# Fifteen half-size groups instead of twelve, the plain down products behind them, and the table sums as accumulating transfers

## The chip, the core and the metric

One core of a Trainium2 chip runs the whole program: TensorE (PE) multiplies, VectorE (DVE), ScalarE (ACT) and GpSimd (POOL) prepare and take away, SyncE (SP) and ACT issue transfers. The metric is the device time of one execution in microseconds. The kernel before takes 3717.69 us (median of 3 runs, 3717.36 to 3717.88).

## The reference, cut to what matters

Two encoder layers over 512 tokens of width 1024. Each has a token mixer (Fourier branch, attention, gates), which the change leaves alone, and a retrieval layer of 16,384 single-neuron experts, which it touches:

```python
def peer_ffn(x, w_query, sub_keys, u_tab, v_tab):
    ...
        q = (xc @ w_query).reshape(-1, PEER_HEADS, 2, PEER_HALF)
        ...
        gate = jax.nn.softmax(sv, axis=-1)
        u = u_tab[eidx]
        act = jax.nn.gelu(jnp.einsum('thkd,td->thk', u, xc), approximate=False)
        w = gate.astype(act.dtype) * act
        vv = v_tab[eidx]
        return jnp.einsum('thk,thkd->td', w, vv)
...
x = layer_norm(DEEPNORM_ALPHA * x + y_p, ln2_g[l], ln2_b[l])
```

## The kernel before, in words

The experts are computed densely. The gates of all heads are summed into a dense array (token by expert), which goes to DRAM. Then, for 32 groups of 512 experts, the kernel forms u·x ("up"), applies gelu, multiplies by the gates ("weights" of the group) and multiplies by the rows of v ("down"), which are added into X. Every 32-bit operand is split into a high and a low part, and a product is three matmuls: high by high, high by low, low by high (`product`, L1561 to L1563). POOL makes the low parts of the tables (L506), the high parts too where nobody else does (L518); in the stages around the gates ACT makes the high parts. A table "piece" is 1 MB; two landing tiles and two pairs `part_h`, `part_l` are used in turn, each in two halves.

Order of one layer's expert work on PE:

1. Early up products (`early_product`): their gelu goes to DRAM (`early_acts`). There are EG = 18 groups of them, 36 pieces: 16 before the dense gates, 16 woven into them (`dense_gates`, 8 blocks), and 4 after them (E_AFTER).
2. Plain down products of 17 of those 18 groups: DVE multiplies `acts_in` by `gate` (`weigh`, L1337), ACT rounds (L846), DVE takes the low part (L1341), PE does 2 halves of 48 matmuls, and DVE adds each pair of banks into X (`add_up`, L1358). The first such group multiplies X by alpha in the same instruction (L1355).
3. One group with up and down products, then SG = 12 "seven" groups (`seven_group`): the up product of the next group, and a down product by Winograd's variant of Strassen's scheme: the 512 x 512 by 512 x 1024 product is cut in blocks of half size, and seven products (P1, P2, P3, P5, P4, P7, P6) of 12 matmuls each take the place of eight. The four sums of table blocks are made by POOL (`table_sum`, L559) in `vraw`, in place; the sums of the weights by DVE. Results go to X or to four accumulators `acc` (`add_seven`, L1443).
4. `gather_seven` adds the accumulators into X in eight steps (L1491, L1494), beside the up product of one more group; the last down product and the layer norm follow.

Everything is in program order on each engine and tied by counting semaphores (`Tally`); `used` counts pieces that PE is through with, `y_added` the bank pairs that DVE has added, `t_added` the table sums, `s_bank` the weight banks that are free again.

Of the kernel before, what the change touches and what calls it, by code (L numbers as in the profile page):

```python
# [5 lines left out]
F32 = mybir.dt.float32  # L6
# [7 lines left out]
P = 128  # L14
# [18 lines left out]
CG = 4  # L33
# [7 lines left out]
EG = 18  # L41
E_BEFORE, E_AFTER = 16, 4
E_WITHIN = 2 * EG - E_BEFORE - E_AFTER
# [19 lines left out]

SG = NG - EG - 2
S_FIRST = P_UV + 4
S_UV = S_FIRST + 2 * SG
S_LAST = S_UV + 4
NS = S_LAST + 2
assert SG % 2 == 0 and NS == NP - 2 * SG
# [49 lines left out]
def build(nc, x, stream, keys, ln0, ln1, ln2, qk_gain, gate_bias, consts, out):  # L119
    ctx = ExitStack()  # L120
    with ctx:
# [97 lines left out]
        raw_h = overlay("raw_h", 56, [P, 2, 3, 2, HALF], F32R)  # L219
        raw_l = overlay("raw_l", 68, [P, 2, 3, 2, HALF], F32R)  # L220
# [3 lines left out]
        end_h = [overlay(f"end_h{i}", kib, [P, CG, S], F32R) for i, kib in enumerate((0, 80))]  # L224
        end_l = [overlay(f"end_l{i}", kib, [P, CG, S], F32R) for i, kib in enumerate((8, 88))]
# [21 lines left out]
        Wh = overlay("Wh", 16, [P, 2, CG, S], F32R)  # L247
        Wl = overlay("Wl", 32, [P, 2, CG, S], F32R)
        gate = [overlay(f"gate{i}", 48 + 8 * i, [P, S, CG]) for i in range(2)]
        acts_in = [overlay(f"acts_in{i}", 72 + 8 * i, [P, CG, S]) for i in range(2)]  # L250
# [75 lines left out]
        spilled = [tally(f"spilled{i}", 0, 16 * S // 64) for i in range(2)]  # L326
        gate_in = [tally(f"gate_in{i}", 0, 16 * n) for i, n in enumerate((EG // 2 + NG - EG, EG // 2))]
# [17 lines left out]
        t_added = tally("t_added", 0, 4 * SG)  # L345
# [5 lines left out]
        seven_added = tally("seven_added", 7, 7 * SG)  # L351
        acc_zero = tally("acc_zero", 0, 1)
# [77 lines left out]
        def _(sp):  # L430
# [11 lines left out]
            def rounds(first, end, sevens):  # L442
                with sp.Fori(first, end) as r:
                    for s in range(LANDINGS):

                        sp.wait_ge(split.sem, r * (2 * LANDINGS) + 2 * (s - LANDINGS + 1 - 2 * SG * sevens))
                        sp.dma_start(landing[s][:], flat[r * LANDINGS + s]).then_inc(landed[s], 16)
# [10 lines left out]
            def seven_pieces(l):  # L458
# [10 lines left out]
                sp.wait_ge(used.sem, used.at(l, P_UV))  # L469
                down_piece(0, 0)  # L470
                up_piece(0, 0)
                down_piece(0, 1)
                up_piece(0, 1)
                with sp.Fori(0, SG - 1) as k:
# [5 lines left out]
                    down_piece(k + 1, 1)  # L480

            begin = 1
            for l in range(DEPTH):
                rounds(begin, (l * NP + P_OUT) // LANDINGS, l)
                for n in range(2):
                    wide_rows(l, n)
                rounds((l * NP + P_OUT + 4) // LANDINGS, (l * NP + P_UV + 4) // LANDINGS, l)
                seven_pieces(l)
                begin = (l * NP + V_LAST - 4) // LANDINGS
# [1617 lines left out]
```

## Time and profile before

| | us |
|---|---|
| median of the runs | 3717.69 |
| the profiled execution: its own time | 3718.94 |
| its span, first to last instruction | 3716.7 |
| PE busy | 3671.4 (99%) |
| POOL busy | 2498.0 (67%) |
| DVE busy | 2526.1 (68%) |
| ACT busy | 1150.8 (31%) |

Layer 0's expert work runs as follows: dense gates until 844, plain down products to about 1263, seven groups to 1790, the rest to 1850; layer 1 repeats it 1846 us later. Busy shares say who works; who is waited for has to be read from the waits and from the timeline of single instructions. The records of matmuls overlap, so a matmul's cost is read from the distance of two starts, not from its length.

### The profile page before, as it was taken

To read this page: it belongs to the slowest core of one execution; us is meant where nothing else is said; L and a number is where in the kernel's file an instruction comes from. 1 tells how busy PE (TensorE), PEld (TensorE's weight loads), DVE (VectorE), ACT (ScalarE), POOL (GpSimd) and SP (SyncE) were. 2 spreads that over 40 slices of the span, in tenths; PEclk is the share of its full clock that TensorE was granted. 3 is DMA by queue.
4 is the path that set the end of the run, shared out by engine and by line. 5 is a ranking of instruction groups with operands and counts; after the bars stand their busy time and mean duration, and the time that the engine had idled before them with its cause. 6 is when DMAs were issued, how large, how long until landed. Compare 5 with 4: busy or idle time off the path is not lost.

```text
span 3716.7 us, 53645 instructions
## 1 busy us (share of the span) xinstructions
PE 3671.4 (99%) x18336; PEld 3032.3 (82%) x18336; DVE 2526.1 (68%) x4281; ACT 1150.8 (31%) x1725; POOL 2498.0 (67%) x1124
## 2 busy tenths in 40 slices
PE   8999999999999999999999999999999999999998
PEld 7778888888888888888887788888888888888886
DVE  7545999994777555555675469999857775555546
ACT  1651134541111134444125412344511111444431
POOL 6445554336777699999764455543377776999995
PEclk9999999999999999999999999999999999999999
DMA  4122245886545433333221223368865553334332
GB/s 154 69 69 103 103 144 176 244 247 247 206 183 192 158 125 113 130 148 117 91 104 69 80 92 113 139 192 243 245 244 191 195 200 136 114 133 148 113 124 79
DMA packets 230084, 555.03 MB, mean 149 GB/s; under 512 B 10048, under 2 KB 141376, under 8 KB 181440
## 3 DMA queue, kind: packets, MB, share of 16 engines
q1 hardware_dynamic: 47968, 337.14, 25.6%
q10 hardware_dynamic: 181984, 216.17, 17.3%
q8 instruction: 78, 1.28, 0.1%
q14 instruction: 54, 0.44, 0.0%
HBM read 446.32 MB, written 106.95 MB: 149 GB/s over the span
## 4 chain that ended last, share of the span: by engine, by line
PE 94%; DVE 3%; POOL 2%; issue 1%; ACT 0%; DMA 0%; POOLq 0%; DVEq 0%; ACTq 0%
PE bank L1561 29%; PE bank L1562 29%; PE bank L1563 29%; PE bank L1890 2%; PE bank L1891 2%; POOL part_l L506 1%; PE bank L1687 1%; PE bank L1850 1%; PE bank L1675 1%; POOL part_h L518 1%; DVE X L1013 1%; DVE X L1015 1%; PE bank L1666 0%; PE bank L1667 0%; DVE stats L999 0%
## 5 line engine op out<-in xcount | busy, mean ns | idle before, releaser
L506 POOL TENSOR_TENSOR part_l<-landing,part_h 128x1024 fp32r<-128x1024 f32 x536 | 1414.6, 2646 | 531.4 <-ACT part_h L766 454.7
L1561 PE MATMUL bank<-XTh,part_h 128*128 128x512 f32 (+1 forms) x2688 | 1047.4, 390 | 5.3 <-ACT Gf L661 2.9
L1563 PE MATMUL bank<-XTh,part_l 128*128 128x512 f32 (+1 forms) x2688 | 1034.1, 385 | 0.0
L1562 PE MATMUL bank<-XTl,part_h 128*128 128x512 f32 (+1 forms) x2688 | 1034.0, 385 | 0.0
L518 POOL TENSOR_SCALAR part_h<-landing 128x1024 fp32r<-128x1024 f32 x316 | 418.1, 1323 | 598.1 <-PE bank L1563 456.5
L1561 PEld LDWEIGHTS bank<-XTh,part_h 128*128 128x128 f32 x2688 | 505.2, 188 | 104.1 <-ACT Gf L661 3.8
L1563 PEld LDWEIGHTS bank<-XTh,part_l 128*128 128x128 f32 x2688 | 505.1, 188 | 101.6
L1562 PEld LDWEIGHTS bank<-XTl,part_h 128*128 128x128 f32 x2688 | 505.6, 188 | 95.5
L552 POOL TENSOR_TENSOR part_l<-vraw,part_h 128x1024 fp32r<-128x1024 f32 x168 | 420.4, 2529 | 42.7 <-ACT part_h L897 42.7
L1561 PE MATMUL bank<-part_h,Wh 128*128 128x512 f32 x1152 | 448.1, 389 | 0.0
L1562 PE MATMUL bank<-part_l,Wh 128*128 128x512 f32 x1152 | 448.1, 389 | 0.0
L1563 PE MATMUL bank<-part_h,Wl 128*128 128x512 f32 x1152 | 448.1, 389 | 0.0
L1337 DVE TENSOR_TENSOR bank<-acts_in,gate 128x512 f32<-128x512 f32 x144 | 302.2, 2144 | 66.0 <-DMA acts_in<-early_acts 58.6
L1358 DVE TENSOR_TENSOR X<-X,bank 128x512 f32<-128x512 f32 x288 | 184.1, 681 | 209.9 <-PE bank L1563 209.9
L846 ACT CAST Wh<-bank 128x512 fp32r<-128x512 f32 x144 | 84.4, 588 | 657.6 <-DVE bank L1337 649.1
L1562 PEld LDWEIGHTS bank<-part_l,Wh 128*128 128x128 f32 x1152 | 216.2, 188 | 45.2
L1563 PEld LDWEIGHTS bank<-part_h,Wl 128*128 128x128 f32 x1152 | 216.2, 188 | 44.8
L1561 PEld LDWEIGHTS bank<-part_h,Wh 128*128 128x128 f32 x1152 | 216.2, 188 | 44.7
L897 ACT CAST part_h<-vraw 128x1024 fp32r<-128x1024 f32 x168 | 170.9, 1044 | 248.4 <-POOL vraw L559 198.5
L755 ACT ACTIVATE early<-bank 128x512 f32<-128x512 f32 x144 | 86.3, 599 | 367.8 <-PE bank L1563 327.1
L1380 DVE TENSOR_TENSOR bank<-bank,gate 128x512 f32<-128x512 f32 x64 | 69.2, 1084 | 188.0 <-ACT bank L870 188.0
L559 POOL TENSOR_TENSOR vraw<-vraw,vraw 128x1024 f32<-128x1024 f32 x72 | 192.0, 2666 | 3.4
(214 smaller groups left out, 5904.0 us busy)
## 6 DMA issues: line engine op xcount, KB each, us to landing
landing<-stream SPq DMA_DIRECT2D x268, 1024.0 KB, 4.8
dense_gates<-spill ACTq DMA_DIRECT2D x32, 2048.0 KB, 9.3
gate<-dense_gates ACTq DMA_DIRECT2D x64, 1024.0 KB, 5.1
vraw<-stream SPq DMA_DIRECT2D x48, 1024.0 KB, 5.1
early_acts<-early ACTq DMA_DIRECT2D x144, 256.0 KB, 2.5
acts_in<-early_acts ACTq DMA_DIRECT2D x36, 1024.0 KB, 7.5
LNP<-ln ACTq DMA_DIRECT2D x4, 1024.0 KB, 5.9
X<-x SPq DMA_DIRECT2D x4, 512.0 KB, 7.3
```

The source lines that it names most:

```text
L506: nc.gpsimd.tensor_tensor(halves(part_l[s], h), halves(landing[s], h), halves(part_h[s], h).bitcast(F32), ALU.subtract).then_inc(split.sem, 1)
L518: nc.gpsimd.tensor_scalar(halves(part_h[s], h), halves(landing[s], h), 1.0, 0.0, ALU.mult, ALU.add).then_inc(high_part.sem, 1)
L552: nc.gpsimd.tensor_tensor(unit(part_l, i), block_of(*UNIT_BLOCK[i]), unit(part_h, i).bitcast(F32), ALU.subtract).then_inc(v_low.sem, 1)
L559: nc.gpsimd.tensor_tensor(block_of(*out), block_of(*left), block_of(*right), ALU.subtract).then_inc(t_added.sem, 1)
L755: nc.scalar.activation(early[:, slot, :], bank[slot][:], ACT.Gelu).then_inc(early_out.sem, 1)
L846: nc.scalar.copy(Wh[:, par, c, :], bank[first_bank + c][:]).then_inc(w_high.sem, 1)
L897: nc.scalar.copy(unit(part_h, i), block_of(*UNIT_BLOCK[i])).then_inc(v_high.sem, 1)
L1337: nc.vector.tensor_tensor(w, acts_in[par][:, c, :], gate[par][:, :, c], ALU.mult).then_inc(w_full.sem, 1)
L1358: ins = nc.vector.tensor_tensor(xs, xs, new, ALU.add)
L1561: nc.tensor.matmul(dst, sth, mvh, start=first, stop=False)
L1562: nc.tensor.matmul(dst, sth, mvl, start=False, stop=False)
L1563: return nc.tensor.matmul(dst, stl, mvh, start=False, stop=last)
```

## The change

EG becomes 16, E_AFTER goes, SG becomes 15. After the dense gates PE does the up product of the first seven group, then the fifteen seven groups, then all 17 plain down products (the group whose up product came last, the 16 early ones). The gates' first load, the alpha scaling of X (now four ACT instructions) and the seven groups' first tables come right behind the dense gates. The four table sums become DMAs from POOL with `accum_op=ALU.add`; so that all are additions, ACT turns the sign of two table blocks (`turn_over`), and P2 and P5 are subtracted instead of added. `gather_seven` is split in four parts of two steps, one behind each of the first four plain groups; `add_up` and `down` take the banks in the order 6, 7, 4, 5.

```diff
-EG = 18
-E_BEFORE, E_AFTER = 16, 4
+EG = 16
+E_BEFORE = 16
...
-SG = NG - EG - 2
+SG = NG - EG - 1
...
-                def table_sum(n, lows, out, left, right):
+                def table_sum(n, lows, out, new):
                     pool.wait_ge(v_low.sem, v_low.at(l, 7 * k + lows))
-                    if n > 1:
-                        pool.wait_ge(t_added.sem, t_added.at(l, 4 * k + n - 1))
-                    nc.gpsimd.tensor_tensor(block_of(*out), block_of(*left), block_of(*right),
-                                            ALU.subtract).then_inc(t_added.sem, 1)
+                    if n == 1:
+                        pool.wait_ge(turned.sem, turned.at(l, 2 * k + 2))
+                    else:
+                        pool.wait_ge(t_added.sem, t_added.at(l, 64 * k + 16 * (n - 1)))
+                    pool.sem_inc(went_on, 1)
+                    pool.dma_start(block_of(*out), block_of(*new), accum_op=ALU.add).then_inc(t_added.sem, 16)
...
                 down_low(P1)
                 down_low(P2)
-                pool.wait_ge(v_landed[1].sem, v_landed[1].at(l, 16 * k + 16))
-                table_sum(1, P1 + 1, b11, b12, b11)
-                table_sum(2, P1 + 1, b12, b22, b12)
+                table_sum(1, P1 + 1, b11, b12)
                 down_low(P3)
+                table_sum(2, P3 + 1, b12, b22)
                 down_low(P5)
+                table_sum(3, P3 + 1, b22, b11)
                 up_lows(1)
-                table_sum(3, P3 + 1, b22, b22, b11)
-                table_sum(4, P3 + 1, b21, b22, b21)
+                table_sum(4, P3 + 1, b21, b22)
...
-                for k in range(2):
-                    act.dma_start(gate[k][:], dense[k]).then_inc(gate_in[k].sem, 16)
-                    act.dma_start(acts_in[k][:], ...).then_inc(acts_back[k].sem, 16)
-                for i in range(E_AFTER - 1):
-                    early_piece(E_BEFORE + E_WITHIN + i, 0, True)
+                act.dma_start(gate[0][:], dense[EG]).then_inc(gate_in[0].sem, 16)
+                for slot in range(4):
+                    act.wait_ge(early_saved[slot].sem, early_saved[slot].at(l, 16 * EG))
+                for tb in range(TB):
+                    ins = nc.scalar.activation(X[:, tb, :], X[:, tb, :], ACT.Copy, scale=ALPHA)
+                ins.then_inc(scaled.sem, 1)
...
+                    def turn_over(chunk, half):
+                        block = block_of(chunk, half)
+                        nc.scalar.activation(block, block, ACT.Copy, scale=-1.0).then_inc(turned.sem, 1)
...
                     act.wait_ge(v_landed[0].sem, v_landed[0].at(l, 16 * k + 16))
+                    turn_over(1, 0)
                     down_high(P1)
+                    act.wait_ge(turned.sem, turned.at(l, 2 * k + 1))
                     down_high(P2)
                     activate(k + 1, 0, None)
                     act.wait_ge(v_landed[1].sem, v_landed[1].at(l, 16 * k + 16))
+                    turn_over(0, 1)
                     down_high(P3)
...
-                gather_seven()
...
+                seven_group(SG - 1, 0, True)
+                dve_group(0, 0, (v_low.sem, v_low.at(l, 7 * SG)))
+                gather_seven(0, (0, 1))
+                dve_group(1, 1, (used.sem, used.at(l, S_DOWN + 2)))
+                gather_seven(1, (2, 3))
+                for q in (2, 3):
+                    dve_group(q, q - 2, (used.sem, used.at(l, S_DOWN + 2 * q)))
+                    gather_seven(q, (2 * q, 2 * q + 1))
...
-                down_group(0, 0, P_VA, [])
-                with pe.Fori(0, EG // 2 - 1) as m:
-                    down_group(2 * m + 1, 1, 4 * m + (P_VA + 2))
-                    down_group(2 * m + 2, 0, 4 * m + (P_VA + 4))
-                pe.wait_ge(early_out.sem, early_out.at(l, CG * EG))
-                both_group(EG - 1, Wh[:, 1], Wl[:, 1], P_UV, ...)
+                for half in range(2):
+                    up(half, S_UP + half, half, lambda c: (early_out.sem, early_out.at(l, CG * EG)))
                 with pe.Fori(0, SG // 2) as m:
                     for par in range(2):
                         seven_group(2 * m + par, par)
-                both_group(EG, end_h[0], end_l[0], S_UV, ...)
+                seven_group(SG - 1, 0)
+                down_group(0, end_h, end_l, [(seven_added.sem, seven_added.at(l, 7 * SG - 1 + n)) for n in range(2)])
+                down_group(1, Wh[0], Wl[0])
+                with pe.Fori(1, EG // 2) as m:
+                    for par in (1, 0):
+                        down_group(2 * m + (1 - par), Wh[par], Wl[par])
```

POOL in a seven group before (vraw0 holds blocks b11 and b21, vraw1 holds b12 and b22; a row with `part_l` is a low part, one with `vraw` on the left a table sum):

```order
L552 TENSOR_TENSOR part_l1<-vraw0_98,part_h1 128x1024 [waits v_high]
L567 ISA
L559 TENSOR_TENSOR vraw0_98<-vraw1_99,vraw0_98 128x2x512 [waits v_low,v_landed1]
L559 TENSOR_TENSOR vraw1_99<-vraw1_99 128x2x512 [waits t_added,v_low]
...
L552 TENSOR_TENSOR part_l0<-vraw0_98,part_h0 128x1024 [waits v_high]
...
L506 TENSOR_TENSOR part_l1<-landing1,part_h1 128x1024 [waits u_high]
L559 TENSOR_TENSOR vraw1_99<-vraw1_99,vraw0_98 128x2x512 [waits t_added,v_low]
L559 TENSOR_TENSOR vraw0_98<-vraw1_99,vraw0_98 128x2x512 [waits t_added,v_low]
```

The same place now:

```order
L571 TENSOR_TENSOR part_l1<-vraw0_98,part_h1 128x1024 [waits v_high]
L577 ISA [waits v_low]
L581 DMA vraw0_98<-vraw1_99 128x2x512 [waits turned]
...
L571 TENSOR_TENSOR part_l0<-vraw1_99,part_h0 128x1024 [waits v_high]
L579 ISA [waits v_low]
L581 DMA vraw1_99<-vraw1_99 128x2x512 [waits t_added]
...
L571 TENSOR_TENSOR part_l0<-vraw0_98,part_h0 128x1024 [waits v_high]
L579 REGISTER_ALU [waits v_low]
L581 DMA vraw1_99<-vraw0_98 128x2x512 [waits t_added]
...
L581 DMA vraw0_98<-vraw1_99 128x2x512 [waits t_added]
```

Each sum now stands behind a wait for the transfer before it, with POOL's own low parts between them.

DVE at the second of the plain groups behind the seven groups, now (rows `X<-X,bank` are `add_up`, `bank<-acts_in,gate` are `weigh`, rows with `acc` on the right the gathering); it starts with the last pair of banks of the group before:

```order
L1367 TENSOR_TENSOR X<-X,bank4 128x512 [waits used]
L1367 TENSOR_TENSOR X<-X,bank5 128x512
...
L1505 TENSOR_TENSOR acc3_103<-acc3_103,acc0_100 128x1024 [waits y_added,seven_added]
L1505 TENSOR_TENSOR acc2_102<-acc2_102,acc3_103 128x1024 [waits acc_step]
L1350 TENSOR_TENSOR bank0<-acts_in1_128,gate1_126 128x512 [waits acc_step,used,acts_back1,gate_in1]
L1350 TENSOR_TENSOR bank1<-acts_in1_128,gate1_126 128x512
...
L1354 TENSOR_TENSOR Wl1_124<-bank0,Wh1_122 128x512 [waits w_high]
...
L1367 TENSOR_TENSOR X<-X,bank6 128x512 [waits v_first,y_added]
```

In a plain group before nothing stood between the two kinds of rows:

```order
L1358 TENSOR_TENSOR X<-X,bank 128x512 x2
L1337 TENSOR_TENSOR bank<-acts_in_126,gate_124 128x512 x2
L1340 ISA
L1341 TENSOR_TENSOR Wl<-bank,Wh 128x512
L1340 ISA
L1341 TENSOR_TENSOR Wl<-bank,Wh 128x512
```

Two gathering rows now stand ahead of the first `weigh` of each of four groups, and the add of banks 6 and 7 stands behind that `weigh`.

## Rows read from the trace of the kernel before

**Rows 1.** The page: busy time, share and instructions of each engine.

```profile
PE 3671.4 (99%) x18336; PEld 3032.3 (82%) x18336; DVE 2526.1 (68%) x4281; ACT 1150.8 (31%) x1725; POOL 2498.0 (67%) x1124
```

**Rows 2.** Waits of PE: line, waited for: us in total, times, longest.

```profile
PE bank L1574 <- DMA C<-consts: 12.2, 1, 12.2
...
PE bank L1561 <- POOL part_l L506: 2.9, 6, 0.9
```

**Rows 3.** Stretches: PE, PEld, DVE, ACT, POOL busy, clock, DMA share, GB/s.

```profile
900.00:1270.00 370.00, 370.00 (x1634) 306.39 (x1633) 264.32 (x268) 39.95 (x68) 288.99 (x137) 1.00 0.51 186
1300.00:1785.00 485.00, 485.00 (x2141) 401.62 (x2140) 254.16 (x395) 197.02 (x248) 444.26 (x179) 1.00 0.33 123
```

**Rows 4.** Timeline, PE, a seven group's start: start, us, what.

```profile
1504.90 0.39 PE L1561 MATMUL bank<-XTh,part_h 128*128 128x512 f32 x1
...
1515.78 0.39 PE L1561 MATMUL bank<-part_h,raw_h 128*128 128x512 f32 x1
```

**Rows 5.** Timeline, POOL, the same group.

```profile
1506.44 5.69 POOL L552 TENSOR_TENSOR part_l<-vraw,part_h 128x1024 fp32r<-128x1024 f32 x2 [0.54 <-ACT part_h L897]
...
1526.46 5.73 POOL L559 TENSOR_TENSOR vraw<-vraw,vraw 128x1024 f32<-128x1024 f32 x2
1533.36 7.13 POOL L552 TENSOR_TENSOR part_l<-vraw,part_h 128x1024 fp32r<-128x1024 f32 x3 [1.16 <-ACT part_h L897]
```

**Rows 6.** Timeline, ACT, the same group.

```profile
1505.32 2.00 ACT L897 CAST part_h<-vraw 128x1024 fp32r<-128x1024 f32 x2 [1.88 <-PE bank L1563]
1510.54 0.58 ACT L870 ACTIVATE bank<-bank 128x512 f32<-128x512 f32 x1 [3.22 <-PE bank L1563]
```

**Rows 7.** DMA issues: count, KB each, median us to landing.

```profile
landing<-stream SPq DMA_DIRECT2D x268, 1024.0 KB, 4.8
...
vraw<-stream SPq DMA_DIRECT2D x48, 1024.0 KB, 5.1
...
out<-X SPq DMA_DIRECT2D x4, 512.0 KB, 2.7
```

**Rows 8.** Timeline, ACT, end of the dense gates of layer 0.

```profile
844.14 0.60 ACT L755 ACTIVATE early<-bank 128x512 f32<-128x512 f32 x1 [2.17 <-PE bank L1563]
...
845.53 0.39 ACTq L818 DMA_DIRECT2D dense_gates<-spill  x1
...
855.22 0.36 ACTq L836 DMA_DIRECT2D gate<-dense_gates  x1
855.61 0.46 ACTq L837 DMA_DIRECT2D acts_in<-early_acts  x1
```

**Rows 9.** Timeline, DVE, the same place.

```profile
863.67 2.05 DVE L1337 TENSOR_TENSOR bank<-acts_in,gate 128x512 f32<-128x512 f32 x2 [29.00 <-DMA acts_in<-early_acts]
```

**Rows 10.** Timeline, DVE, one half of a plain down group.

```profile
1061.74 1.28 DVE L1358 TENSOR_TENSOR X<-X,bank 128x512 f32<-128x512 f32 x2 [2.88 <-PE bank L1563]
1062.94 4.27 DVE L1337 TENSOR_TENSOR bank<-acts_in,gate 128x512 f32<-128x512 f32 x2
1067.12 1.44 DVE L1341 TENSOR_TENSOR Wl<-bank,Wh 128x512 fp32r<-128x512 f32 x2
1068.48 1.28 DVE L1358 TENSOR_TENSOR X<-X,bank 128x512 f32<-128x512 f32 x2
```

**Rows 11.** Timeline, DVE, the gathering behind the seven groups.

```profile
1792.02 1.42 DVE L1494 TENSOR_TENSOR acc<-acc,acc 128x1024 f32<-128x1024 f32 x1
1793.47 1.96 DVE L1491 TENSOR_TENSOR X<-X,acc 128x1024 f32<-128x1024 f32 x1
1795.35 3.41 DVE L1491 TENSOR_TENSOR acc<-acc,acc 128x1024 f32<-128x1024 f32 x1
1798.68 12.70 DVE L1491 TENSOR_TENSOR X<-X,acc 128x1024 f32<-128x1024 f32 x5
```

**Rows 12.** Timeline, DVE, a seven group's weights times gates.

```profile
1511.15 0.62 DVE L1389 TENSOR_TENSOR sum_of<-bank,gate 128x256 f32<-128x256 f32 x1 [3.63 <-ACT bank L870]
...
1516.59 1.10 DVE L1380 TENSOR_TENSOR bank<-bank,gate 128x512 f32<-128x512 f32 x1 [3.83 <-ACT bank L870]
...
1520.35 0.42 DVE L1403 TENSOR_TENSOR sum_of<-sum_of,bank 128x256 f32<-128x256 f32 x1
```

More of the change, by code:

```diff
@@ L467, in down_piece, with plain_piece @@
                                  flat[4 * k + (l * NP + P_UV + 5 + 2 * s)]).then_inc(v_landed[s].sem, 16)
[L469 to L473, printed above, removed]
+                def plain_piece(n, s, piece):
+                    sp.wait_ge(split.sem, split.at(l, 2 * (n + s - LANDINGS + 1)))
+                    sp.dma_start(landing[s][:], flat[l * NP + piece]).then_inc(landed[s], 16)
+                for s in range(2):
+                    plain_piece(S_UP, s, P_UV + 2 * s)
+                for s in range(2):
+                    up_piece(0, s)
+                for s in range(2):
+                    sp.wait_ge(spilled[s].sem, spilled[s].at(l, 16 * (S // 64)))
+                for s in range(2):
+                    down_piece(0, s)
                 with sp.Fori(0, SG - 1) as k:
@@ L614, in xt_parts @@
                                    bank[banks[i]][:].rearrange("p (k t) -> p k t", k=4)).then_inc(xt_high.sem, 1)
+            for k in range(2):
+                act.sem_inc(spilled[k].sem, 16)
             root(1, slice(0, 2))
@@ L1461, in seven_group @@
                     if last:
[L1462 removed]
+                        end_lows(0)
                     else:
@@ L1514, in _ @@
-                dve.wait_ge(used.sem, used.at(l, P_UV))
+                    dve.wait_ge(seven_added.sem, seven_added.at(l, 7 * SG))
+                    dve.wait_ge(y_added.sem, y_added.at(l, 4 * group + 4))
+                    for n in steps:
+                        dst, new = [(p6, p1), (p7, p6), (x11, p1), (x12, p6), (x21, p7), (x22, p7), (x12, p5),
+                                    (x22, p5)][n]
+                        if n > 0:
+                            dve.wait_ge(acc_step.sem, acc_step.at(l, n))
+                        nc.vector.tensor_tensor(dst, dst, new, ALU.add).then_inc(acc_step.sem, 1)
@@ L1515, in _ @@
+                    dve.wait_ge(acc_step.sem, acc_step.at(l, steps[-1] + 1))
+                    dve.sem_inc(went_on, 1)
+                for k in range(2):
+                    dve.wait_ge(spilled[k].sem, spilled[k].at(l, 16 * (S // 64)))
+                for i in range(4):
+                    ins = nc.vector.memset(acc[i][:], 0.0)
+                ins.then_inc(acc_zero.sem, 1)
                 for p in range(2):
```

298 lines of the change are left out of this document (120 added, 178 removed).

## The prediction, made before the run

> **What bounds the kernel now.** I read the page's busy times first: PE is busy 99% of the span, no other engine over 68% [rows 1]. Then PE's waits: the longest is the start's wait for the constants, and for POOL's low parts it waits 2.9 us in all [rows 2]. Then the stretches: in the plain down products and in the seven groups alike PE is busy all the time at the full granted clock, while POOL works 92% of the seven groups' stretch (444 of 485 us) and 78% of the plain one's (289 of 370), and DVE 52% and 71% [rows 3]. So the end is set by PE's row of matmuls, and a change pays by the matmuls that it takes away, as long as every operand keeps arriving in time. The timelines of single instructions are for that second half: how early each operand is there.
>
> **What it removes.** From one seven group's first up matmul (1504.90) to its first P1 matmul (1515.78) are 48 matmuls: 10.88 / 48 = 0.2267 us each [rows 4]. A plain down product has 96 of them, a seven group's has 7 x 12 = 84. Three more groups in each of two layers take away 3 x 2 x 12 = 72 matmuls: 16.3 us. Up products and everything else on PE keep their number.
>
> **The four sums as transfers, in a group that runs steadily.** Times from here count from the group's first up matmul. PE does up (48 matmuls) to 10.9, P1, P2, P3 and P5 (2.72 each) to 21.8, up again to 32.65, then P4, P7 and P6 to 40.8. P4 needs the fourth sum. Before, POOL had the sums done at 27.3 (1526.46 + 5.73) and the low part of P4 at about 30.9 [rows 5], 1.8 us ahead of need. Now ACT first turns a block, 1.0 us like its cast of the same size, so P1's cast ends at 0.42 + 2.0 = 2.4 [rows 6]. Two low parts of 2.4 follow on POOL (7.13 for three in a row [rows 5]), and the second turn, behind the gelu that starts at 5.6, ends at 7.2 [rows 6]: the first sum is issued at 7.4. Each later one is issued when the one before has landed. From the fourth landing to P4's low part it is a cast and a low part, 3.5 with the hand-overs. With L for a transfer from issue to landing, 0.4 for the hand-overs, and 1.5 more for the fourth, which meets the landing of the next 1 MB piece, the condition is 7.4 + 4L + 1.9 + 3.5 <= 32.65, so L <= 4.96 us. Every us above costs 4 us in each of 30 groups, 120 us. Nothing like this transfer is in the trace of before. The nearest rows are 512 KB written out in 2.7 us and 1 MB loaded in 4.8 and 5.1 [rows 7]. An accumulating transfer must read the new block and the old one, 1 MB, and write 512 KB. The bounds are 2.7 (it costs nothing) and something above 5.1 by POOL's own issue: I put 6 as the upper end, one of the 1 MB rows and some 0.9 for an issue that no row shows. I take 4.8, the row nearest to it in bytes read. Then P4 is ready at 32.0, 0.65 us ahead: nothing in the steady group. Lower ends below zero are excluded, since PE does not wait there now. The up product's second piece is next: POOL comes to its low part after the third issue, 7.4 + 2 x 4.9 + 1 = 18.2, and has it at 20.6, needed at 21.8. The freed time of POOL (4 x 2.4 us in each group) buys nothing, since nobody waited for POOL. ACT's two turns are 2 us of 40.8 on an engine that was busy 41% [rows 3] and are hidden but for the place counted above. P5's low part ends at 7.4 + 4.8 + 3.5 = 15.8, needed at 19.05.
>
> The Trainium skill ("DMA: Bandwidth & Descriptors", Anatomy of one DMA) gives for a POOL-issued DMA 2.0 us plus bytes over 436 GB/s; with 1 MB read that is an estimate of 4.4 us, inside the budget, and the forecast stays. The same page's table (Bandwidth, measured) has 6.15 us of transfer time alone for 1 MB on that path, which no run here shows yet; by it the steady group would be 4.8 us late and the kernel some 143 us slower than my sum, the first rival below.
>
> **Behind the dense gates.** Before, four early pieces (43.5 us of PE) covered the way of the gates to DRAM and back. Now PE has 96 matmuls, 21.8 us. Layer 0, absolute times:
> - The up product waits for all early gelus. The last starts at 844.14 and takes 0.60 [rows 8]: PE stands from about 843.95 to 844.9, 0.95 us, and is through with both up pieces at 866.7.
> - The spill is issued at 845.53 and its landing lets the gate load go at 855.22 [rows 8], the same now. With it SP now issues two `vraw` loads of 1 MB, which need the same landing. Before, the second of the four loads issued there took from 855.61 to 863.6 (DVE's wait ends at 863.67 [rows 9]), so I let the gate land at 863.4; alone it would be at 860.3. The alpha scalings of X, 4 x 1.0 on ACT, end at 859.7 and lie beside that, and so do the memsets.
> - DVE then needs 2 x 0.62 for the first chunk, 1.10 for the second and four sums of 0.42 [rows 12], 4.0; high and low parts of the bank on ACT and DVE take it to 869.4 (2.0, from casts and low parts of 0.4 to 0.7 for such sizes, half of the 1.44 for two in [rows 10]). PE stands 2.7 us.
> - The first seven group lacks its lead: the second pair of chunks takes ACT and DVE until 877, only then come turn, cast and low part of P1, ready at 881.8 where PE wants it at 880.3 (1.5 us). The first sum is issued at 884.3, that is 14.9 after the group's start instead of 7.4. P3 costs 0.5 more, P5 (landing 889.1, ready 892.6) 2.2, the second up piece (behind the third issue) 2.1, P4 1.4: 7.7 us. In the next group the lag is gone.
> That is 11.4 us a layer. The lower end is 1.5 (gate at 860.3, L of 2.7), the upper 18 (L of 6).
>
> **The gathering inside the plain groups.** In a plain half DVE starts with the last pair of banks at 1061.74, weighs (4.27), takes low parts, and has added the next pair at 1068.48 + 1.28 = 1069.8, when PE wants it at 1061.6 + 10.88 = 1072.5 [rows 10]: 2.7 us of slack. Two gathering steps now stand ahead of that. They took 1.42 and 3.41 for the accumulators, 1.96 and 12.70 / 5 = 2.54 for X [rows 11]: 4.8, 4.5, 5.1 and 5.1 for the four pairs. PE then waits 2.1, 1.8, 2.4 and 2.4 us for banks 6 and 7 in the middle of four groups: 8.7 us a layer. If the steps run at the 1.42 of the quickest, it is 0.1 each; if all at 3.41, 16. Before, they lay beside an up product that needed none of these banks. PE's first plain group has 1.4 us to the second half of its first table piece, like the up product before; I count no difference.
>
> **The sum.** Own time of the profiled execution 3718.94 (span 3716.7 and 2.2 around it), -16.3, +2 x 11.4, +2 x 8.7: 3742.8. That execution is 1.25 above the median, so 3742. This measurement can tell a change from none at about 0.2%, 7.4 us.
>
> **Rivals.**
> 1. *The transfers are too slow.* L of 5.8 (1 MB load and an issue): P4 is late by 4 x 0.84 = 3.4 us in 30 groups, 101 us: 3843. For it: four in a row that each wait for the one before, in a group that had 1.8 us to spare. Against it: three of the four lie where no load is in flight. It decides from 4.96 us. The 6.15 of the page named above would give 3885.
> 2. *The covers hold, and it is faster.* DVE and POOL slow each other now (a low part takes 2.4 alone, 3.3 beside DVE [rows 5]); if POOL, freed of the sums and standing between pieces, leaves the gathering at 1.42 a step, and L is near the 2.7 of the 512 KB row, then what is left is 0.95 + 0.5 behind the gates and 0.4 of gathering in each layer: 3718.9 - 16.3 + 3.7 - 1.25 = 3705. It decides where waits come to under 8.9 us in all (16.3 - 7.4).
> 3. *Half of it.* The steps are as quick as in 2 but the first seven group starts late as I count it, or the reverse: 16 us of waits, 3718.
>
> **How the numbers follow.** Forecast 0.37, own range 3728 to 3758; rival 1 0.32; rival 2 0.20; rival 3 0.11. Faster by over 0.2%: 0.20; within: 0.11; slower: 0.69. The range leaves out the last us of rival 2 and the part of rival 1 above L of 5.8: 3706 to 3840.
>
> **What would show it.** Right: PE's waits name ACT's early gelu (0.9 a layer), DVE's `raw_l` (2 to 3) and POOL's `part_l` from `vraw` (some 8 a layer, all in the first group); in the middle of four plain groups PE waits about 2 us for DVE's add of banks 6 and 7; seven groups still follow each other every 40.8 us; the POOL transfers land in 4.4 to 5.0 us. Wrong: a period above 40.9 (rival 1, and the landing time gives it), no wait in the gathering groups, or a gate that lands within 5 us of its issue.

## The result and the profile after

The changed kernel takes 3957.72 us (median of 4 runs, 3957.36 to 3964.36), the kernel before 3717.53 beside it (3716.99 to 3717.88): a ratio of 1.065, 95% interval 1.063 to 1.067. It is 240 us slower. I had forecast 3742 and a range up to 3840, so the time lies outside. The profile is that of the slowest of the four executions (3964.36).

The page's first part of the changed kernel (busy us, share, instructions), which answers to [rows 1]:

```profile
PE 3745.0 (95%) x18264; PEld 3061.4 (77%) x18264; DVE 2609.1 (66%) x4389; ACT 1284.4 (32%) x1871; POOL 2332.3 (59%) x1118
```

PE has the 72 matmuls less that I counted (18336 to 18264), and yet its busy time rises by 74 us: some matmuls take longer. Its share falls from 99% to 95%. The waits of PE (total us, times, longest), which answer to [rows 2]:

```profile
PE bank L1555 <- POOL part_l L571: 118.9, 32, 4.0
PE bank L1555 <- POOL part_l L525: 30.1, 38, 4.6
PE bank L1555 <- DVE X L1367: 22.6, 8, 2.9
...
PE bank L1555 <- DVE raw_l L1421: 5.5, 2, 2.9
...
PE bank L1555 <- ACT early L775: 1.4, 2, 0.7
```

L571 is the low part of a block of v (plain or summed), L525 that of an up piece, L1367 the adding of banks to X. The first row has 32 waits for 30 groups: one for P4 in every seven group, which I had forecast free of waits in the steady group, and two for P5 in the first group of each layer. A stretch of the seven groups of layer 0 (PE, PEld, DVE, ACT, POOL, clock, DMA share, GB/s), which answers to the second of [rows 3]:

```profile
1100.00:1200.00 100.00, 87.17 (x362) 70.39 (x362) 46.58 (x71) 40.97 (x51) 64.78 (x32) 0.95 0.55 147
```

PE stands 13 of 100 us, with POOL down from 92% to 65%, and the clock below 1.00 for the first time. One group of those, on POOL (start, us, what, idle time before), which answers to [rows 5]; PE begins this group at 1113.80:

```profile
1116.29 4.77 POOL L571 TENSOR_TENSOR part_l<-vraw,part_h 128x1024 fp32r<-128x1024 f32 x2 [1.49 <-ACT part_h L909]
1121.56 1.20 POOL L581 DMA_DIRECT2D vraw<-vraw  x1 [0.50 <-POOL part_l L571]
1122.33 2.84 POOL L571 TENSOR_TENSOR part_l<-vraw,part_h 128x1024 fp32r<-128x1024 f32 x1
1127.17 1.20 POOL L581 DMA_DIRECT2D vraw<-vraw  x1 [2.00 <-DMA vraw<-vraw]
1127.95 2.87 POOL L571 TENSOR_TENSOR part_l<-vraw,part_h 128x1024 fp32r<-128x1024 f32 x1
1132.76 1.20 POOL L581 DMA_DIRECT2D vraw<-vraw  x1 [1.95 <-DMA vraw<-vraw]
1133.54 5.19 POOL L525 TENSOR_TENSOR part_l<-landing,part_h 128x1024 fp32r<-128x1024 f32 x2
1138.32 1.57 POOL L581 DMA_DIRECT2D vraw<-vraw  x1
1148.97 7.03 POOL L571 TENSOR_TENSOR part_l<-vraw,part_h 128x1024 fp32r<-128x1024 f32 x3 [9.07 <-ACT part_h L909]
```

The four rows of L581 are the transfers. They are issued 5.61, 5.59 and 5.56 us apart, each when the one before has landed. The fourth is issued at 1138.32, and what it lets go on ACT starts only 9.5 us later. SP's queue and ACT's timeline of the same group:

```profile
1138.90 0.33 SPq L470 DMA_DIRECT2D landing<-stream  x1
```

```profile
1147.83 1.99 ACT L909 CAST part_h<-vraw 128x1024 fp32r<-128x1024 f32 x2 [14.92 <-DMA vraw<-vraw]
```

SP issued the next 1 MB piece 0.58 us behind the fourth transfer. On PE, same group:

```profile
1147.23 0.39 PE L1557 MATMUL bank<-XTh,part_l 128*128 128x512 f32 x1
1151.46 0.79 PE L1555 MATMUL bank<-part_h,raw_h 128*128 128x512 f32 x1 [3.83 <-POOL part_l L571]
1152.05 0.63 PE L1556 MATMUL bank<-part_l,raw_h 128*128 128x512 f32 x1
1152.47 0.63 PE L1557 MATMUL bank<-part_h,raw_l 128*128 128x512 f32 x1
...
1156.59 0.39 PE L1555 MATMUL bank<-part_h,sum_h 128*128 128x512 f32 x1
```

P4 starts at 1151.46, where PE wanted it at 1147.46, and then its twelve matmuls start 0.43 us apart instead of 0.23. The same stretch by windows (columns as above):

```profile
1147.60:1151.40 3.80, 0.02 (x1) 0.00 (x0) 1.06 (x2) 3.57 (x5) 2.43 (x2) 0.76 0.00 0
1151.50:1156.20 4.70, 4.70 (x11) 3.74 (x12) 2.71 (x5) 0.25 (x1) 4.49 (x2) 0.50 0.58 223
1156.50:1162.00 5.50, 5.50 (x26) 4.54 (x25) 3.69 (x6) 3.80 (x5) 3.75 (x2) 1.00 0.85 328
```

After PE stood for 3.8 us the granted clock is 0.50, that is 1.2 GHz, for 4.7 us, and then 1.00 again. A late operand costs twice: the wait of 4.0, and the slow matmuls (1151.46 to 1156.59 is 5.13 for twelve starts instead of 12 x 0.2267 = 2.72), 2.4. In 8 of the 30 groups all twelve matmuls are slow like this; in the other 22 it is seven or eight of them, some starting only after a few at full rate, 1.6 us. Over the 30 groups that is 54 us. With 0.9 for the up product's second piece this group is some 7 us too long: groups of layer 0 begin at 923.17 and, six later, at 1209.62, so one takes 47.7, against the 40.8 of before.

The DMA rows of the changed kernel, which answer to [rows 7] (count, KB each, median us to landing):

```profile
landing<-stream SPq DMA_DIRECT2D x256, 1024.0 KB, 5.0
...
gate<-dense_gates ACTq DMA_DIRECT2D x64, 1024.0 KB, 6.3
vraw<-stream SPq DMA_DIRECT2D x60, 1024.0 KB, 4.9
vraw<-vraw POOLq DMA_DIRECT2D x120, 512.0 KB, 5.0
```

The median of 5.0 is that of three in four. The fourth is told by the timeline alone.

### The profile page after: what moved, and what is told of

Same layout as the page of the kernel before. It is cut to its first block and busy times, and to the rows that moved or that the text cites. A ratio compares the mean times of both kernels' runs of the same rounds, so it can differ in the third digit from the quotient of the medians.

```text
span 3962.4 us, 53991 instructions
## 1 busy us (share of the span) xinstructions
PE 3745.0 (95%) x18264; PEld 3061.4 (77%) x18264; DVE 2609.1 (66%) x4389; ACT 1284.4 (32%) x1871; POOL 2332.3 (59%) x1118
## 5 line engine op out<-in xcount | busy, mean ns | idle before, releaser
L525 POOL TENSOR_TENSOR part_l<-landing,part_h 128x1024 fp32r<-128x1024 f32 x512 | 1354.2, 2678 | 550.6 <-ACT part_h L786 456.6
L571 POOL TENSOR_TENSOR part_l<-vraw,part_h 128x1024 fp32r<-128x1024 f32 x210 | 525.0, 2514 | 337.4 <-ACT part_h L909 337.4
L537 POOL TENSOR_SCALAR part_h<-landing 128x1024 fp32r<-128x1024 f32 x268 | 347.9, 1298 | 570.4 <-PE bank L1557 423.5
L1555 PE MATMUL bank<-part_h,Wh 128*128 128x512 f32 x1024 | 402.9, 394 | 23.5 <-DVE X L1367 22.6
L1557 PE MATMUL bank<-part_h,Wl 128*128 128x512 f32 x1024 | 401.5, 392 | 0.0
L1556 PE MATMUL bank<-part_l,Wh 128*128 128x512 f32 x1024 | 401.4, 392 | 0.0
L909 ACT CAST part_h<-vraw 128x1024 fp32r<-128x1024 f32 x210 | 212.5, 1039 | 497.3 <-DMA vraw<-vraw 497.3
L1367 DVE TENSOR_TENSOR X<-X,bank 128x512 f32<-128x512 f32 x256 | 163.1, 681 | 170.1 <-PE bank L1557 170.0
L1555 PE MATMUL bank<-part_h,raw_h 128*128 128x512 f32 x360 | 163.2, 453 | 114.1 <-POOL part_l L571 114.1
L1555 PEld LDWEIGHTS bank<-part_h,Wh 128*128 128x128 f32 x1024 | 194.0, 189 | 68.3 <-issue 25.9
L1451 DVE TENSOR_TENSOR acc<-acc,bank 128x512 f32<-128x512 f32 x240 | 154.1, 683 | 132.4 <-PE bank L1557 132.4
L581 POOL DMA_DIRECT2D vraw<-vraw x120 | 154.3, 1286 | 132.3 <-DMA vraw<-vraw 118.9
L1557 PEld LDWEIGHTS bank<-part_h,Wl 128*128 128x128 f32 x1024 | 194.0, 189 | 40.8
```

What stands on the lines that cost most here:

```text
L525: nc.gpsimd.tensor_tensor(halves(part_l[s], h), halves(landing[s], h), halves(part_h[s], h).bitcast(F32), ALU.subtract).then_inc(split.sem, 1)
L537: nc.gpsimd.tensor_scalar(halves(part_h[s], h), halves(landing[s], h), 1.0, 0.0, ALU.mult, ALU.add).then_inc(high_part.sem, 1)
L571: nc.gpsimd.tensor_tensor(unit(part_l, i), block_of(*UNIT_BLOCK[i]), unit(part_h, i).bitcast(F32), ALU.subtract).then_inc(v_low.sem, 1)
L581: pool.dma_start(block_of(*out), block_of(*new), accum_op=ALU.add).then_inc(t_added.sem, 16)
L909: nc.scalar.copy(unit(part_h, i), block_of(*UNIT_BLOCK[i])).then_inc(v_high.sem, 1)
L1367: ins = nc.vector.tensor_tensor(xs, xs, new, ALU.add)
```

## The experiments

Theory A: the transfers make nearly all of the loss, as a chain, and within it the fourth, which shares the DMA engines with SP's load. Theory B (the main rival): it is the order around them, the fifteenth group and what stands behind the gates. Each run computes the whole reference. Times are medians; a ratio is against the kernel before, run beside it (medians of 3717.4 to 3718.3).

**The load behind the fourth transfer.** SP waits for the fourth sum before it loads the up piece's second half.

```diff
                     up_piece(k + 1, 0)
+                    sp.wait_ge(t_added.sem, t_added.at(l, 64 * k + 64))
                     up_piece(k + 1, 1)
```

> The changed kernel, with SP's load of the next group's second up piece held back until the fourth table sum has landed. Theory A (the fourth transfer takes 9.5 us instead of 5.0 because that 1 MB load is issued in the same microsecond and shares the DMA engines): the fourth lands in 5 to 6 us, P4's low part is there 3.8 us earlier, PE's wait for it falls to 0.5 us or less, the slow matmuls behind it go too, and a seven group takes 41 to 41.5 us instead of 47.6: 3957.7 less some 30 x 6.2 = 3770 to 3790 us. Theory B (the fourth is slow by itself, for its blocks or its place behind POOL's low parts): it still lands after 9.5 us, a group stays at 47.6 us and the time within 10 us of 3957.7.

3799.96 us, ratio 1.022 (1.020 to 1.024): 157.8 us less, 10 us short of what theory A gave. Timelines of POOL, ACT and SP of that run:

```profile
1025.90 1.52 POOL L582 DMA_DIRECT2D vraw<-vraw  x1
```

```profile
1031.27 2.00 ACT L910 CAST part_h<-vraw 128x1024 fp32r<-128x1024 f32 x2 [10.72 <-DMA vraw<-vraw]
```

```profile
1031.50 0.33 SPq L470 DMA_DIRECT2D landing<-stream  x1
```

The fourth transfer now lands in 5.4 (1025.90 to 1031.27), like the others, and the P4 wait is gone from 28 of the 30 groups, but for 0.7 us in one. In the last group of each layer another line of SP issues the load (L478), which the edit does not hold back, and there the wait stays (3.7 and 3.9 us). What is left in the steady group is a wait at the up product's second half, PE's waits in that run:

```profile
PE bank L1556 <- POOL part_l L526: 24.5, 36, 1.5
PE bank L1556 <- DVE X L1368: 22.6, 8, 2.9
PE bank L1556 <- POOL part_l L572: 13.7, 7, 3.9
```

The group takes 41.9 us, 1.1 more than before. So the collision in these 28 groups cost 158 of the 240 us, with the slow matmuls behind it. The Trainium skill ("DMA: Bandwidth & Descriptors", Issuing engines are not separate DMA queues) has all issuers' transfers on the same DMA engines, where they interleave; the two traces agree: the fourth transfer took 9.5 us beside the load against 5.4 before it, and the load 6.3 beside the transfer, where the load ahead of the first transfer in the same group took 4.8.

**The sums back on POOL, all else as changed.**

```diff
-                    pool.sem_inc(went_on, 1)
-                    pool.dma_start(block_of(*out), block_of(*new), accum_op=ALU.add).then_inc(t_added.sem, 16)
+                    nc.gpsimd.tensor_tensor(block_of(*out), block_of(*out), block_of(*new),
+                                            ALU.add).then_inc(t_added.sem, 16)
```

> The changed kernel, with the four table sums as POOL additions again (same order, same turned blocks). Theory A (the transfers cost all of the seven groups' 6.8 us; the gathering and the start behind the dense gates cost what the trace of the changed kernel shows, with the slow matmuls behind each wait): seven groups every 40.8 to 41.2 us, PE waits for DVE's add of banks 6 and 7 stay at 2.8 us eight times with some 1.8 us of slow matmuls each (37 us), the start costs 7 to 9 us a layer: 3718.9 - 16 + 37 + 16 = 3750 to 3760 us. Rival (fifteen groups and the turned blocks cost something of their own in the seven groups): groups above 42 us, 3790 or more.

3763.70 us, ratio 1.012 (1.011 to 1.014): the transfers cost 194 us. The time is 4 us above theory A's range; the rival's groups above 42 us did not come (41.1). The other 46 us stay without any transfer. The largest part is PE's first wait, 22.7 us, with the slow matmuls behind it; six of its eight places have them, 1.6 us each:

```profile
PE bank L1555 <- DVE X L1367: 22.7, 8, 3.0
...
PE bank L1555 <- DVE raw_l L1421: 4.5, 2, 2.5
```

**The transfers alone, in the kernel before.** The order of before with its 12 groups a layer; the sums, the two turned blocks and their sign as in the change.

```diff
-                    nc.gpsimd.tensor_tensor(block_of(*out), block_of(*left), block_of(*right),
-                                            ALU.subtract).then_inc(t_added.sem, 1)
+                    pool.sem_inc(went_on, 1)
+                    pool.dma_start(block_of(*out), block_of(*new), accum_op=ALU.add).then_inc(t_added.sem, 16)
...
+                    turn_over(1, 0)
...
+                    turn_over(0, 1)
```

> The kernel before with one part of the change alone: the two turned blocks and the four table sums as accumulating transfers; still twelve seven groups, their order and everything else as before. Theory A (the chain of four transfers, the fourth beside a 1 MB load, makes every seven group 47.6 us instead of 40.8, whatever stands around them): 24 groups x 6.8 = 163 us more, 3870 to 3890 us. Rival (the chain is only late because the first group behind the dense gates starts without a lead and the lag is handed on): groups near 41 us, 3720 to 3740.

3881.36 us, ratio 1.043 (1.042 to 1.045). That is 163.8 us over 24 groups, 6.8 a group, where the changed kernel has 47.74 - 40.8 = 6.9. PE's waits:

```profile
PE bank L1570 <- POOL part_l L553: 88.3, 24, 4.1
```

24 waits for 24 groups, 3.7 each. The cost belongs to the transfers in a group of this length, not to the fifteen groups or to what stands behind them; theory B falls for all but the 46 us.

**The clock behind a wait.** If the slow matmuls come from PE's standing, they go when PE has something to do. Ahead of P4, PE does 14 matmuls more, into the bank that P4 then overwrites.

```diff
+                    if i == P4:
+                        pe.wait_ge(seven_added.sem, seven_added.at(l, 7 * k + (i - 1)))
+                        for _ in range(14):
+                            nc.tensor.matmul(bank[4 + 2 * ((par + i) % 2)][:], XTh[:, 0, 0:P], XTl[:, 0, :],
+                                             start=True, stop=True)
                     pe.wait_ge(v_low.sem, v_low.at(l, 7 * k + (i + 1)))
```

> The changed kernel, with 14 matmuls that nobody needs (3.2 us) put on PE ahead of the wait for P4's table block, into the bank that P4's product then overwrites. Theory A (behind a PE wait of 3.8 us the granted clock halves for the next 8 to 12 matmuls, 2 us more): P4 starts at the same time as in the changed kernel, its matmuls follow every 0.227 us, a seven group takes about 45.4 us instead of 47.6 and the kernel 60 to 70 us less, near 3890. Theory B (these matmuls are slow for their operands, or the clock falls anyway): no gain, 3950 to 3970 us.

3913.12 us, ratio 1.053 (1.051 to 1.054): 44.6 us less (I had expected 60 to 70), with the operand as late as before. PE's timeline and one window (clock in the third last column):

```profile
1139.32 3.33 PE L1942 MATMUL bank<-XTl,XTh 128*128 128x512 f32 x14
...
1143.15 0.50 PE L1555 MATMUL bank<-part_h,raw_h 128*128 128x512 f32 x1 [0.49 <-POOL part_l L571]
```

```profile
1143.20:1148.00 4.80, 4.80 (x21) 3.97 (x22) 4.42 (x9) 2.06 (x5) 4.80 (x3) 1.00 0.83 246
```

No matmul starts 0.43 apart behind the wait and the clock stays at 1.00. The seven groups' 26 whole periods are 45.92 us in the mean, against 47.75 in the changed kernel: 1.83 less, 55 in thirty groups, which is the 54 of slow matmuls. The two profiled executions differ by 52.9 (spans 3909.5 and 3962.4). The medians differ by less since the profiled execution of the changed kernel is 6.6 above its median.

**The gathering, spread.** The sums on POOL as above, and one gathering step behind each half of a plain group instead of two behind a whole one.

```diff
...
                     add_up(q, 0, 2 * q + (S_DOWN + 1))
+                    if gather:
+                        gather_seven(4 * q + 2, (2 * q,))
                     weigh(q, par, 1)
                     add_up(q, 1, 2 * q + (S_DOWN + 2))
+                    if gather:
+                        gather_seven(4 * q + 4, (2 * q + 1,))
...
```

> The kernel with the sums on POOL, and the gathering spread: one of the eight steps behind each half of the first four plain groups instead of two behind each group. Theory A (PE waits in the middle of these groups since two steps, 4.5 to 5 us, stand before an add with 2.7 us of slack): single steps of 1.4 to 3.4 us mostly fit, the eight waits of 2.8 us fall below 0.5 us each and the slow matmuls with them, 30 to 37 us less than the kernel with the sums on POOL: about 3720. Rival (these waits come from POOL and DVE slowing each other in that stretch, not from the order): at most 10 us less.

3747.28 us, ratio 1.008 (1.006 to 1.009): 16.4 less than with the two steps together. That is neither the 30 to 37 of theory A nor the rival's 10 at most. The changed kernel's timelines show the two steps on DVE (5.37 us ahead of the weighing) and then PE's wait:

```profile
1641.84 5.37 DVE L1505 TENSOR_TENSOR X<-X,acc 128x1024 f32<-128x1024 f32 x2
1647.60 3.77 DVE L1350 TENSOR_TENSOR bank<-acts_in,gate 128x512 f32<-128x512 f32 x2 [0.39 <-DVE X L1505]
```

```profile
1654.10 0.49 PE L1555 MATMUL bank<-part_h,Wh 128*128 128x512 f32 x1 [2.80 <-DVE X L1367]
...
1655.02 0.63 PE L1555 MATMUL bank<-part_h,Wh 128*128 128x512 f32 x1
```

and with the steps spread, waits, timeline and window of PE:

```profile
PE bank L1556 <- DVE X L1367: 13.7, 8, 1.7
```

```profile
1541.37 0.49 PE L1556 MATMUL bank<-part_h,Wh 128*128 128x512 f32 x1 [1.72 <-DVE X L1367]
```

```profile
1541.60:1545.00 3.40, 3.40 (x16) 2.79 (x16) 2.91 (x4) 0.00 (x0) 3.40 (x2) 1.00 0.97 383
```

The waits fall by 9 us, the time by 16. Of the eight waits of 2.8 in the run with both steps together, six have matmuls 0.43 apart behind them (9.4 us in all); behind the eight of 1.7 there are none and the clock stays at 1.00. So the rest of the gain, 7 us, is the clock that did not fall.

**The gathering between two adds.** As above, but the step stands between the adds of a half's first and second pair of banks.

```diff
...
                     for n, s in enumerate((1, 0)):
+                        if n == 1 and step is not None:
+                            gather_seven(4 * group + 2 * half + 1, (step,))
...
```

> The changed kernel with the sums on POOL (3763.7 us), and each of the eight gathering steps put between the adds of the two bank pairs of one half, where DVE sat idle for 2.9 us in the plain groups of the kernel before. Theory A: a step of 1.4 to 3.4 us fits that idle time, DVE's waiting falls instead of PE's growing; PE's eight waits of 2.8 us and the slow matmuls behind them go, 33 to 37 us less: 3726 to 3731 us. Rival (DVE and POOL are so much slower together that any place costs): waits of 1 us and more stay, 3740 or more.

3728.73 us, ratio 1.003 (1.002 to 1.004): 35.0 less than with two steps behind each group, and no wait for L1367's X is left in PE's row of the plain groups. There DVE had time: it waited for the banks anyway. The same run has a wait of only 1.84 us with slow matmuls behind it (layer 1, behind the gates; then a window, columns as above):

```profile
2720.01 0.50 PE L1554 MATMUL bank<-XTh,part_h 128*128 128x512 f32 x1 [1.84 <-DVE raw_l L1423]
```

```profile
2721.60:2725.00 3.40, 3.40 (x10) 2.67 (x9) 3.26 (x7) 0.00 (x0) 0.00 (x0) 0.52 0.16 67
```

**Gates first.** SP waits for the first gate before it loads table blocks.

```diff
+                sp.wait_ge(gate_in[0].sem, gate_in[0].at(l, 16))
                 for s in range(2):
```

> The kernel with the sums on POOL, turned blocks and the gathering in DVE's idle time (3728.7 us), with one thing more: the first two v blocks are loaded behind the first gates instead of beside them. Theory: the gates land in about 5 us instead of 7 to 8, PE's wait of 2.5 us for the first free banks and the 1.8 us of slow matmuls behind it go: 6 to 8 us less, 3721 to 3723. The rest down to the 3716.0 of the kernel without turned blocks is then the turning. Rival (the gate load was slow for its own reasons): no change, and the turning cost all 12.7 us.

3724.16 us, ratio 1.0017 (1.0008 to 1.0027, 10 runs): 4.6 less, where 6 to 8 were expected; DVE's `raw_l` is no longer among what PE waits for.

**The fifteen groups with the sums of before.** No turned blocks, POOL's order and subtractions as before, with both edits above.

```diff
-                table_sum(1, P1 + 1, b11, b12)
+                pool.wait_ge(v_landed[1].sem, v_landed[1].at(l, 16 * k + 16))
+                table_sum(1, P1 + 1, b11, b12, b11)
+                table_sum(2, P1 + 1, b12, b22, b12)
                 down_low(P3)
-                table_sum(2, P3 + 1, b12, b22)
                 down_low(P5)
-                table_sum(3, P3 + 1, b22, b11)
                 up_lows(1)
-                table_sum(4, P3 + 1, b21, b22)
+                table_sum(3, P3 + 1, b22, b22, b11)
+                table_sum(4, P3 + 1, b21, b22, b21)
```

> Only the order of the change: fifteen seven groups with all plain groups behind, the table sums exactly as before (POOL subtractions, no turned blocks), the gathering steps in DVE's idle time as in the run beside it, and the first two table blocks of v loaded after the first gates have landed. Theory A: 72 matmuls less are worth 16 us; what is left against it is the wait for the last early gelu (1.3 us a layer), a shorter wait for the first gates (0 to 1 us instead of 2.6 and 1.8 of slow matmuls) and 1 to 4 us in the first seven group: 3718 - 16 + 6 to 12 = 3707 to 3714, faster than both kernels. Rival (a first group without lead costs what the fifteen groups give): 3716 to 3722.

3716.03 us, ratio 0.9994 (0.9985 to 1.0003, 11 runs): as before, though 16.3 us of matmuls are gone, and in the rival's range. The turned blocks and the order of the sums that came with them cost 8 us (0.2 in each steady group: 41.03 against 40.80); no run has one without the other. PE's waits show what eats the rest:

```profile
PE bank L1551 <- POOL part_l L572: 7.1, 2, 3.7
```

Two waits, one a layer: the first group's P3, which has no lead, with seven to nine slow matmuls behind each.

**Two orders of POOL's row.** First the second sum behind the up pieces:

```diff
-                table_sum(2, P1 + 1, b12, b22, b12)
                 down_low(P3)
                 down_low(P5)
                 up_lows(1)
+                table_sum(2, P1 + 1, b12, b22, b12)
```

> The kernel with fifteen groups and the sums as before, with POOL's order changed: first sum, low parts of P3, P5 and the up piece, then the other three sums. Theory: the first seven group's wait for P3 (3.7 us and 1.6 us of slow matmuls a layer) shrinks to about 1.6 us since P3's low part comes 2.4 us earlier, P4 may be late by 1.5 us instead in that one group, and the steady groups keep their 40.8 us since P4's low part still ends at about 31 of 32.65 us: 3 us a layer less, 3708 to 3712 us, below both kernels. Rival (the sums behind the low parts make P4 late in every group): groups of 41.2 us and more, 3722 or above.

3741.84 us, ratio 1.0064 (1.0050 to 1.0077). My theory failed and the rival's range held: three sums in a row behind the up pieces bring P4 0.7 us late in each steady group, which takes 41.8:

```profile
PE bank L1551 <- POOL part_l L572: 25.3, 30, 2.2
```

Then P3's low part ahead of the second sum:

```diff
-                table_sum(2, P1 + 1, b12, b22, b12)
                 down_low(P3)
+                table_sum(2, P1 + 1, b12, b22, b12)
```

> The same base (3716.0 us) with POOL's low part of P3 ahead of the second table sum only, so that nothing stands idle in a steady group. Theory: P3 of the first seven group comes 2.4 us earlier and P5 is then late by about 2 us: 3.3 us of waits in place of 3.7 and 1.6 of slow matmuls, 2 to 4 us less in all, 3712 to 3714; steady groups stay at 40.8 us. Rival (the wait only moves to P5 and the clock falls there): no change, 3715 to 3717.

3711.85 us, ratio 0.9985 (0.9976 to 0.9994, 11 runs). Its interval overlaps that of the run that it changes, so what it gains there (4 us) isn't settled; its first group waits 1.2 for P3 and 1.7 for P5 in layer 0, without slow matmuls behind.

**A lead for the first group.** ACT casts the first group's P1 and P2 as soon as the first pair of banks is through, ahead of the second pair.

```diff
...
                     sum_highs(0, p)
+                    if p == 0:
+                        act.wait_ge(seven_done.sem, seven_done.at(l, 0))
+                        act.wait_ge(used.sem, used.at(l, S_FIRST))
+                        act.wait_ge(v_landed[0].sem, v_landed[0].at(l, 16))
+                        down_high(P1)
+                        down_high(P2)
...
```

> The kernel with fifteen groups and the sums as before (3716.0 us), with the first seven group given its lead back: ACT's casts of its P1 and P2 blocks come ahead of its gelus, casts and sums for the second pair of weight banks, as soon as the up piece has left the part tiles. POOL's row then starts some 6 us earlier in that group. Theory (what is left against fifteen groups is this group's late start, 3.7 us of wait and 1.6 us of slow matmuls a layer): both go, up to 10 us less, 3705 to 3710 us, below both kernels. Rival (the second pair of banks, now 2 us later, becomes what PE waits for): 3712 to 3716.

3703.95 us (3703.44 to 3704.84), ratio 0.9962 (0.9949 to 0.9976): 13.6 us under the kernel before (14.0 under the 3717.98 beside it), the fastest of all. The two long waits are gone, and PE is busy 99%:

```profile
PE bank L1560 <- POOL part_l L526: 5.3, 9, 1.2
```

**The transfers with all of this.** Load behind the fourth transfer, gathering between adds, gates first, and the low part of the up piece's first half ahead of the third transfer.

```diff
+                pool.wait_ge(u_high.sem, u_high.at(l, 4 * k + 3))
+                low_half(1, 0)
                 table_sum(3, P3 + 1, b22, b11)
-                up_lows(1)
+                pool.wait_ge(u_high.sem, u_high.at(l, 4 * k + 4))
+                low_half(1, 1)
                 table_sum(4, P3 + 1, b21, b22)
```

> The changed kernel with its transfers kept, fitted in: the next piece's load behind the fourth transfer, the low part of the up piece's first half ahead of the third transfer, the gathering in DVE's idle time and the v blocks behind the first gates. Theory A (of the 82 us that the kernel with only the load moved is above the one before, 37 are the gathering, about 30 are PE's waits of 0.6 us and their slow starts for the up piece in each group, the rest the start): 3725 to 3745 us. If the chain then ends at the fourth transfer all the same, PE's waits move to P4's low part and the groups stay at 41.9 us: 3755 to 3765.

3755.12 us, ratio 1.010 (1.009 to 1.012). The up piece is in time, P4 is now 0.8 late in each group:

```profile
PE bank L1559 <- POOL part_l L573: 35.0, 36, 2.7
```

and the group stays at 41.9, as the second half of the expectation had it. Four transfers of 5 us one behind the other did not fit into a group of 40.8 in either of the two orders tried.

## Why the prediction was wrong

The parts, each as the difference of two runs (us):

| part | us | from |
|---|---|---|
| matmuls less and what remains, against before | -13.6 | first-group lead run |
| first group without a lead | +12.1 | lead removed |
| turned blocks, with POOL's order of the sums | +8.1 | fifteen groups to gates first |
| table loads ahead of the gates | +4.6 | gates first to gathering between adds |
| gathering behind whole groups | +35.0 | to sums on POOL |
| transfers | +194.0 | to the changed kernel |
| sum | +240.2 | |

- **Matmuls less.** Right: 72 fewer, 16.3 us by count, and 13.6 measured once everything else was out of the way.
- **The transfers: the step that failed.** "L for a transfer from issue to landing, 0.4 for the hand-overs, and 1.5 more for the fourth." L of 4.8 was near: 5.0 measured (the 4.4 and the 6.15 us quoted beside my sum were both further off). The other two terms were mis-sized. The hand-overs were 0.6 each, not 0.1, since landing, POOL's wait and the issue follow one another: the fourth issue came 24.5 us into the group, not 22.1. And the fourth took 9.5 where I gave 6.3 (4.8 + 1.5, with a hand-over 6.4). I had named the meeting with the 1 MB landing, but no row stood behind the 1.5; here the transfer and the load, started within 0.6 us of each other, were through after about the sum of both alone (5.0 + 4.8), and it was the transfer that came last. With 0.1 behind the landing that is 5.6 us: P4 came 37.7 into the group, against 32.0 forecast and 32.65 needed. PE wanted it at 33.7 by then, 0.9 of that being its own wait for the up piece, which was late from the same spacing. Without the meeting the measured terms still give 7.8 + 3 x 5.6 + 5.4 + 3.6 = 33.6, 0.9 late: the chain did not fit even so, as the groups of 41.9 in the first run show.
- **Rival 1** was the mechanism, with the right place. It gave 101 us for L of 5.8 in all four, where 194 were measured from three of 5.0 and one of 9.5; its argument against itself ("three of the four lie where no load is in flight") looked at the three that did not matter.
- **The clock** was in no term, and without it the waits alone would not make the 240 us. In the changed kernel all 30 waits for P4, five of the eight in the gathering and all four for `raw_l` and P5 behind the gates were followed by some 7 to 12 matmuls at 1.2 GHz, 1.4 to 2.4 us. That is 54 us in the steady and first groups at P4, 8 in the gathering and 6 behind the gates, in the profiled execution.
- **The gathering.** Cause, place and wait right: 2.8 in each of 8 places against 1.8 to 2.4 forecast, 22.6 us against 17.4. But undoing it gave 35.0: 9.4 of the 12 more are the slow matmuls.
- **Behind the gates.** Early gelu 0.7 a layer (forecast 0.95), `raw_l` 2.75 (2.7): these held. In layer 0's first group POOL's low parts came late for P5 by 2.5 (2.2) and for the up piece by 0.9 (2.1), for P1 and P3 not at all (1.5 and 0.5). P4's 3.7 (1.4; my own terms, added up again, give 0.6) is the collision. So the cause and the place held, and without P4 the late start cost 3.4 a layer where I gave 6.3, with 1.6 of slow matmuls behind `raw_l` and again behind P5 that I had not counted.
- **What I did not see.** ACT's two turned blocks, counted as hidden, and the order that puts three sums instead of two ahead of the up piece's low parts cost 8 us together. Which of the two does it stays open.

## What to carry to other kernels

A chain of dependent transfers is priced by its last link, at the moment at which that link runs: look at what the other queues issue in the same microsecond, and, until a run says otherwise, take the sum of both durations, which was right here. A wait on PE of some us can cost more than its length (1.6 to 2.4 us more behind 3.8 here), and if it cannot be avoided, work of any kind on PE in its place gives part of it back. When an edit pays little, first look at what the engine with time to spare is waiting for anyway: moving the gathering from behind a group into the gap between two adds gave back 35 us.

## What the runs showed of the hardware

- **An accumulating transfer of 512 KB within SBUF, issued by POOL.** 5.0 us from issue to landing alone, 9.5 with a 1 MB load issued 0.6 us later, which itself took 6.3 instead of 4.8. An issue has 1.20 us in POOL's row (1.57 at the fourth); POOL's next low part starts after 0.77 already, but then takes 2.84 where one takes 2.39 (4.77 / 2). A POOL sum of the same block took 5.73 / 2 = 2.9 [rows 5]: the transfer is the slower of the two and frees POOL for 1.7 us (2.9 - 1.2).
- **The granted clock behind a wait.** It fell behind PE waits of 3.6 to 4 us for P4, in all 30 groups of the changed kernel, to 0.50 in the window read; behind five of its eight waits of 2.8 in the gathering; and not behind waits of 1.7 or 0.7. It came back after 7 to 12 matmuls. The length alone does not decide: in the run with the gathering between two adds the `raw_l` wait of 2.69 in layer 0 was followed by matmuls at full rate, and that of 1.84 in layer 1 by eight slow ones, with the clock at 0.52. What tells these two apart stays open. The Trainium skill ("TensorE: Matmul & The Clock Gate") has the clock drop when PE is idle; the windows above agree, with 0.50 after 3.8 us.
